# A one-core transformer pair on Trainium2: attention values taken one round later, and one projection output moved in front of a norm's sums

## The reference, cut to what matters

```python
def mla_qkv(p, prm, pos):
    q_a, kv_a, k_rope = jnp.split(p, [MLA_Q_RANK, MLA_Q_RANK + MLA_KV_RANK], axis=-1)
    q = (rmsnorm_2(q_a, prm['g_qa']) @ prm['w_q_up']).reshape(B, L, MLA_HEADS, MLA_QK)
    kv = (rmsnorm_2(kv_a, prm['g_kva']) @ prm['w_kv_up']).reshape(B, L, MLA_HEADS, MLA_NOPE + MLA_V)
    ...
def mixer_ab(hc, hl, row, col, need_ctx, prm):
    pc = hc @ prm['w_in']
    pl = hl @ prm['w_in']
    r_c, v_c, dirs_c, g_c = rwkv_prep(pc[..., :RW_COLS], prm)
    ...
    q_l, k_l, vm_l = mla_qkv(pl[..., RW_COLS:], prm, (row, col))
    o_l = latent_attention(q_l, k_l, vm_l, k_c, vm_c, scale)   # softmax(q k^T * scale) v
```

## Time and profile before

| | us |
|---|---|
| median of 3 runs | 2590.62 |
| lowest, highest | 2585.58, 2597.38 |
| profiled execution | 2596.23 |
| its span | 2594.4 |
| TensorE busy | 2379.0 (92%) |
| VectorE busy | 1746.2 (67%) |
| ScalarE busy | 1053.4 (41%) |
| GpSimd busy | 343.0 (13%) |

### The profile page before, as it was taken

How to read it: one execution, slowest core, us unless ns; L and a number is a source line. 1 busy time by engine, 2 the same in 40 slices (tenths; PEclk the granted TensorE clock), 3 DMA queues, 4 the chain that set the end, 5 groups by cost and what they waited for, 6 DMA issues and landing times.

```text
span 2594.4 us, 38771 instructions
## 1 busy us (share of the span) xinstructions
PE 2379.0 (92%) x15040; PEld 1759.5 (68%) x15040; DVE 1746.2 (67%) x3348; ACT 1053.4 (41%) x2064; POOL 343.0 (13%) x534
## 2 busy tenths in 40 slices
PE   7999999799999799889998899988899998898997
PEld 3788888554888699833444577776576776667775
DVE  4875786576746778722657766665678885648985
ACT  4222222233221434421144244443467773446884
POOL 0111110100000011100200233331022210001220
PEclk9999999899999899999999999999999999998998
DMA  8555653231326478511010100000279993115995
GB/s 307 200 196 195 219 195 138 102 138 65 120 69 218 144 270 284 188 41 65 33 41 25 42 2 3 3 2 2 99 266 346 332 319 115 57 65 191 348 326 198
DMA packets 115063, 386.98 MB, mean 149 GB/s; under 512 B 20160, under 2 KB 22336, under 8 KB 114624
## 3 DMA queue, kind: packets, MB, share of 16 engines
q1 hardware_dynamic: 76640, 276.33, 30.3%
q0 software_dynamic: 34848, 95.47, 10.9%
q10 hardware_dynamic: 3392, 12.70, 1.3%
HBM read 389.66 MB, written 26.21 MB: 160 GB/s over the span
## 4 chain that ended last, share of the span: by engine, by line
PE 33%; DVE 14%; DMA 9%; ACT 6%; issue 3%; POOL 0%; DVEq 0%; ACTq 0%; SPq 0%; POOLq 0%
PE ps L143 32%; DMA RG<-in_w 6%; DVE moe0wl L152 2%; DVE moe1wl L152 2%; DMA AR<-in_a 1%; DVE rwMM L172 1%; PE ps L146 1%; DVE f2wl L152 1%; DVE acc L160 1%; ACT moe0wh L149 1%; ACT moe1wh L149 1%; DVE H L160 1%; ACT gqaas L149 1%; DVE rwXF L152 1%; ACT rwWU L149 1%
## 5 line engine op out<-in xcount | busy, mean ns | idle before, releaser
L143 PE MATMUL ps<-H,RG 128*128 128x256 f32 (+2 forms) x1088 | 363.9, 491 | 14.0 <-ACT H L149 14.0
L160 DVE SCALAR_TENSOR_TENSOR acc<-AR,cs,acc 128x512 f32<-128x512 f32 x420 | 295.9, 747 | 44.7 <-DMA AR<-in_a 42.4
L143 PEld LDWEIGHTS ps<-H,RG 128*128 128x128 f32 (+1 forms) x1088 | 206.8, 193 | 156.0 <-issue 139.7
L152 DVE TENSOR_TENSOR moe0wl<-RG,moe0wh 128x1024 fp32r<-128x1024 f32 x144 | 173.3, 1221 | 38.3 <-ACT moe0wh L149 30.0
L149 ACT ACTIVATE moe0wh<-RG 128x1024 fp32r<-128x1024 f32 x144 | 151.1, 1062 | 69.2 <-DMA RG<-in_w 44.4
L199 POOL DMA_DIRECT2D AR<-in_a x152 | 82.4, 542 | 713.2 <-DVE acc L160 520.3
L149 ACT ACTIVATE f1wh<-RG 128x1024 fp32r<-128x1024 f32 x66 | 69.8, 1061 | 228.1 <-PE ps L143 228.0
L152 DVE TENSOR_TENSOR moe1wl<-RG,moe1wh 128x1024 fp32r<-128x1024 f32 x120 | 144.4, 1220 | 25.2 <-ACT moe1wh L149 19.8
L143 PE MATMUL ps<-f1hh,f1wh 128*128 128x512 f32 x352 | 143.2, 407 | 4.8 <-DVE f1hl L152 4.8
L149 ACT ACTIVATE moe1wh<-RG 128x1024 fp32r<-128x1024 f32 x120 | 125.8, 1062 | 49.0 <-DMA RG<-in_w 29.6
L143 PE MATMUL ps<-f1hh,f1wl 128*128 128x512 f32 x352 | 140.4, 399 | 0.0
(11 more groups left out here) (634 smaller groups left out, 5791.4 us busy)
## 6 DMA issues: line engine op xcount, KB each, us to landing
RG<-in_w SPq DMA_DIRECT2D x525, 512.0 KB
AR<-in_a POOLq DMA_DIRECT2D x152, 512.0 KB, 3.7
moe0back<-moe_outs ACTq DMA_DIRECT2D x4, 1024.0 KB, 8.0
CT<-in_consts ACTq DMA_DIRECT2D x1, 2546.0 KB, 14.1
X<-in_x ACTq DMA_DIRECT2D x1, 2048.0 KB, 11.6
moe_rows<-moe0ht POOLq DMA_DIRECT2D x4, 512.0 KB, 5.2
moe1back<-moe_outs ACTq DMA_DIRECT2D x2, 1024.0 KB, 6.0
X<-in_ctx ACTq DMA_DIRECT2D x1, 1024.0 KB, 5.8
```

Of the source, the lines that this page charges most:

```text
L143: return Silent() if self.e is None else self.e.matmul(out, lhs, rhs, start=start, stop=stop, skip_group_check=True)
L152: return Silent() if self.e is None else self.e.tensor_tensor(out, a, b, op)
L160: return Silent() if self.e is None else self.e.scalar_tensor_tensor(out=out, in0=a, scalar=s, in1=b, op0=op0, op1=op1)
```

## The change

The values of pair p stand in round 2p+5, so on odd rounds, and each attention has one more round. ACT's program keeps its order, because it has nothing of V. In mixer 1 that round brings two more fill units, which feed-forward 2 no longer has. In MLA's front output 0 stands between kr and the queries' sums, and output 1 in front of the keys' sums. GQA's leading products have a fourth round in which nothing is led.

```diff
@@ class Attention, parts and rounds @@
-        pair = u - self.LAG - 2
+        pair = u - self.LAG - 3
...
-        return range(2 * self.n + self.LAG + 1)
+        return range(2 * self.n + self.LAG + 2)
@@ Mla.pe @@
+        rw.output_pe(e, 0)
         self.nq.pe(e)
-        rw.output_pe(e, 0)
+        rw.output_pe(e, 1)
         self.nk.pe(e)
-        rw.output_pe(e, 1)
         rw.output_pe(e, 2)
@@ lead_pe @@
-        for k in {first: range(0, 4), first + 1: range(4, 6), first + 2: range(6, 7)}[u]:
+        for k in {first: range(0, 4), first + 1: range(4, 6), first + 2: range(6, 7), first + 3: ()}[u]:
```

## The result

The changed kernel took 2565.02 us (median of 4 runs, 2559.46 to 2568.07) against 2592.13 for the kernel before (4 runs): a ratio of 0.9892, interval 0.9866 to 0.9919. Two further comparisons of the same pair gave 0.9911 (0.9890 to 0.9931) and 0.9904 (0.9882 to 0.9926). In microseconds of 2594 that is 28, 23 and 25 less. Faster was forecast, by 18.5; the time lies within the range of 2560 to 2585, some 7 us beyond the forecast value.

The account below looks back on a forecast made before the run. TensorE was busy for 2379.0 of 2594.4 us, so its waits decide. Gains of 6.6 + 5.4 + 4.2 + 0.9 + 1.4 = 18.5 us take the median from 2590.62 to 2572.1, range 2560 to 2585.

Parts of the forecast that it names:

- The norm: MLA's low-rank norm: output 0 fills TensorE's wait of 4.81 us; gain 6.6 us, bounds 4.8 and 7.3.
- the wait that stays: MLA's norm, before the keys' sums: TensorE still waits 1.3 us, at most 1.45, behind output 1.
- MLA's attention: Waits for RWKV copies (4.2 us) and transposed weights (1.6) go, less 0.4 left: gain 5.4, bounds 3 and 6.5.
- GQA: GQA's attention: a pair of rounds falls from 7.10 to 6.29 us; gain 4.2 after a longer tail, bounds 1.5 and 6.
- The loop: GQA's attention: values wait 0.99 us for ACT, DVE's copy 0.81 for values, and the next maximum stands behind that copy.
- the doubt about the first values' clock: GQA's attention: the first values may run at half clock, 3.68 against 1.95 us, holding DVE up some 2.5.
- The tail: GQA's end: 1.95 us of values product moves behind round 15's transposes, with 0.6 back from round 13's transposes.
- The rival that GQA keeps its pace: GQA's attention: a pair stays at 7.10 us, so GQA gives -1.4 and the total is 2580.1; chance 0.12.
- First mixer: First mixer's attention: the wait of 0.83 us before the last values goes; gain 0.9, bounds 0 and 2.
- DVE's cover: First mixer's scan start: DVE's stand of 11.28 us hides its ending the attention about 3.0 later, at no cost.
- Feed-forward 2: Second feed-forward: two modulation units, 2.73 us of DVE work, leave its DVE-bound start; gain 1.4, between 0 and 2.7.
- The clock rival: GQA's attention: without early values TensorE stays at 1.2 GHz, giving 2616.9 us; chance 0.03.

Follow-up runs that it names:

- run 7: Only MLA's attention takes its values a round later, against the kernel before: ratio 1.0003 (0.9983 to 1.0024).
- before again: The kernel before, profiled a second time with no edit: a single execution of 2601.33 us.
- run 6: Only mixer 1's values a round later, without the extra round's fill units, against the kernel before: ratio 1.0007 (0.9988 to 1.0027).
- run 8: Only GQA's attention takes its values a round later, against the kernel before: ratio 0.9977 (0.9955 to 1.0000).

## Why the prediction was right, and where its sizes were off

**Direction and place: right.** Each place got shorter by about its wait, as its own stage shows in every profile. For the norm and for GQA nothing was seen to be taken back; for MLA alone (run 7) that is not shown.

**The norm: 6.6, measured 7.4** (35.8 to 28.4; 33.0 to 25.7 from kr). The step that was mis-sized is the wait that stays, 1.3 taken and 0.52 measured. I had left the time from the queries' sums to the keys' at 8.32; it is now 1156.24 - 1148.69 = 7.55. In before ACT's copy of output 0, which had to wait for the output's end, stood in front of the keys' square. Moving output 0 forward moved that copy out of the chain. The sums took 2.57 us at a granted clock of 1.00 (2.73 taken) where, behind the wait of 4.81, they had taken 4.38 at 0.60. The run with the norm alone has the same 28.5. This agrees with the Trainium skill, "TensorE: Matmul & The Clock Gate", Part 1, which says that TensorE falls back to 1.2 GHz when it is idle.

**MLA's attention: 5.4, measured 6.3 in the attention.** Behind it, up to the scan, 64.2 on average against 63.8, so 5.8. The waits in the short rounds went altogether, where I had left 0.4.

**GQA: 4.2, measured 4.3 to 6.1** (with before again and before). The loop is gone as argued. The pair of rounds was taken at 6.29 and is 6.21, since the copy of the values costs DVE nothing. From the maxima of round 0 to those of round 15 there are 46.6 us (2216.01 to 2262.60); 48.2 were forecast, and 1.2 of the 1.6 between them were allowed for the doubt about the first values' clock. The tail, from these maxima to the last led product, was forecast at 14.8 and is 2277.07 - 2262.60 = 14.5. The rival that GQA keeps its pace fell.

**First mixer: 0.9, measured 1.3 in the attention at the full clock, and 2.0 more in its end.** DVE's cover was used as forecast (the stand of 11.28 became 7.37; I had said 3.0 less and it is 3.9, of which 1.3 is there without the extra units too, 10.02 in run 6). It cost nothing: TensorE's wait for hge is 2.5 us in the kernel before and in the changed one. The step that failed is the one that priced the two extra units at nothing until feed-forward 2: all units between stand two places earlier too, and a wait of TensorE in mixer 1's end went with that, 1.0 us from m1scr to the norm. The other 1.0 of the end is the half clock in the norm's first 16 records, which mostly came and went with that wait. Beyond this, 0.5 more in the attention on average of all kernels is the clock's. I did not forecast any of it.

**Feed-forward 2: 1.4, measured 1.0 or 1.7 between kernels with the norm's order alike.** The plain difference of the means is 2.3. All are inside the bounds of 0 and 2.7.

Together, as means over all kernels with and without the edit: 1.8 (mixer 1's attention), 2.0 (its end), 2.3, 7.5, 5.8 and 4.7 are 24.1, against 28, 23 and 25 by the ratios. So of the 6 us beyond the forecast about 3 are in mixer 1, half of it clock, 1 is in the feed-forward and not shown to be the units', and the rest are small excesses of the other three. That the sum meets the ratios is in part luck: the scatter of single profiles is as large as these excesses, and MLA's heads, 1.4 to 2.2 us shorter in the changed kernel's profiles, are not in it.

**The clock rival fell.** GQA's start without values kept the full clock up to the first values product in six of the seven profiles that have the new order, and in five of the seven with the old one. In the seventh new one (run 8) the clock fell in round 4 (0.50 from 2245 to 2249, behind a wait of 1.76 us), and was back before the first values:

```profile
2249.25 2.08 PE L143 MATMUL ps<-gqk,gqq 64*128 64x512 f32 x4
2251.26 1.26 PE L146 MATMUL ps<-CT,gqaas 128*128 128x128 f32 x8
2252.45 1.95 PE L143 MATMUL ps<-gqaapt,gqv 128*64 128x256 f32 x16
```

There it cost 0.8 us (54.8 against 54.0), where it had cost 1.8 in front of the values. Scores and transposes together, with no values among them, brought the clock back here. Scores are products, so no run here shows what transposes do by themselves, of which the same page of the Trainium skill speaks in Part 4.

## What to carry to other kernels

When one product waits for a copy that another engine makes, look for work whose inputs are long ready and put it between; the same move may take away a wait that is not the one you aimed at, as the copy of output 0 did here. When a move shifts a counter that spreads background work over stages, follow every later place of that work, not only its last one: here a wait in the stage between went with it. When two sets of kernels are compared by their means, look whether they differ in a second edit as well, as the feed-forward's 2.3 us did. And before explaining a difference of a few microseconds between two profiles, profile both kernels a second time and look whether the stage repeats.

## What was unexpected of the hardware

The same instructions of the same kernel run at a different granted clock from run to run in some stages. Mixer 1's attention took 89.5 and 87.8 us in two profiles of one kernel, GQA's first values product 3.68 and 1.95, and, in two kernels that are alike at that place, an RWKV output behind a row of 0.20 us waits took 9.27 or 7.50. Other stages repeat within 0.1 us, and short waits alone do not tell which: MLA's attention took 88.0 or 88.1 us in the six profiles with later values there, and 94.4 in all eight with the old order, which has six waits of up to 1.1 us in it. The whole kernel before scattered from 2582.0 to 2602.0 us in 35 executions. A single profile of this kernel is therefore good to some 10 us in its span, and to 0.1 us only in stages that were seen to repeat.
